# FFN up projections: 512-column matmuls over high and low activations, halves added on ACT and DVE

## The reference, cut to what matters

```
def swiglu(x, w_gu, w_down):
    g, u = jnp.split(x @ w_gu, 2, axis=-1)
    return (jax.nn.silu(g) * u) @ w_down
...
h = x + 0.5 * swiglu(rmsnorm(x, g[0]), w_ffn_gu[layer, 0], w_ffn_down[layer, 0])
```

## Time and profile before

| | |
|---|---|
| median of 3 runs | 2766.53 us (2764.23 to 2768.34) |
| span of the profiled execution | 2765.9 us |
| PE, PEld busy | 95%, 93% of the span |
| DVE, ACT busy | 66%, 45% |
| matmuls and weight loads | 21248 each |
| weight units | 407, 1 MB each |

### The profile page before, as it was taken

One profiled execution on the slowest core, in us unless ns is written; L12 is line 12 of the kernel. 1 busy time (PEld: TensorE's weight loads), 2 busy tenths in 40 slices (PEclk: granted clock), 3 DMA queues, 4 the chain that ended last, 5 costly groups with the idle time before them and its releaser, 6 DMA issues.

```text
span 2765.9 us, 49966 instructions
## 1 busy us (share of the span) xinstructions
PE 2638.7 (95%) x21248; PEld 2574.0 (93%) x21248; DVE 1820.8 (66%) x2256; ACT 1257.7 (45%) x1323; POOL 5.2 (0%) x13
## 2 busy tenths in 40 slices
PE   8999799999999999999969999999899999899998
PEld 8999799999999999999959999999899998778897
DVE  6567875576566755865676567557876586566565
ACT  4446554454444544544555445446454445333443
POOL 0000000000000000000000000000000000000000
PEclk9999999999999999999989999999999999999999
DMA  7554145545542555455415544554145544123251
GB/s 289 182 182 172 34 174 194 183 161 188 182 174 100 187 183 182 152 197 183 156 61 187 182 168 179 184 182 158 59 172 198 182 168 173 61 91 138 77 183 46
DMA packets 60204, 435.78 MB, mean 158 GB/s; under 512 B 6720, under 2 KB 6848, under 8 KB 7584
## 3 DMA queue, kind: packets, MB, share of 16 engines
q1 hardware_dynamic: 59184, 429.05, 43.3%
q0 software_dynamic: 880, 4.65, 0.5%
HBM read 432.63 MB, written 1.05 MB: 157 GB/s over the span
## 4 chain that ended last, share of the span: by engine, by line
PE 84%; DVE 12%; ACT 2%; issue 1%; DMA 0%; ACTq 0%; DVEq 0%
PE ps L596 56%; PE ps L623 18%; PE ps L609 4%; DVE w_lo L1349 2%; ACT w_hi L996 1%; PE ps L852 1%; DVE xg_lo L1392 1%; PE ps L832 1%; DVE xg_hi L1389 1%; PE ps L842 1%; DVE x L1453 1%; DVE scratch L1623 1%; DVE scratch L1779 1%; DVE scratch L1635 1%; DVE scratch L1613 0%
## 5 line engine op out<-in xcount | busy, mean ns | idle before, releaser
L1349 DVE TENSOR_TENSOR w_lo<-raw,w_hi 128x2048 fp32r<-128x2048 f32 x407 | 932.1, 2291 | 505.1 <-ACT w_hi L996 504.3
L596 PE MATMUL ps<-xg_hi,w_hi 128*128 128x256 f32 x4240 | 1212.5, 286 | 29.2 <-DVE xg_lo L1392 24.7
L596 PE MATMUL ps<-xg_hi,w_lo 128*128 128x256 f32 x4240 | 1201.1, 283 | 0.0
L596 PE MATMUL ps<-xg_lo,w_hi 128*128 128x256 f32 x4240 | 1201.0, 283 | 0.0
L996 ACT CAST w_hi<-raw 128x2048 fp32r<-128x2048 f32 x407 | 772.4, 1898 | 491.9 <-PE ps L623 248.0
L596 PEld LDWEIGHTS ps<-xg_hi,w_hi 128*128 128x128 f32 x4240 | 808.1, 191 | 38.5 <-issue 23.4
L596 PEld LDWEIGHTS ps<-xg_hi,w_lo 128*128 128x128 f32 x4240 | 808.4, 191 | 2.9 <-issue 2.4
L596 PEld LDWEIGHTS ps<-xg_lo,w_hi 128*128 128x128 f32 x4240 | 808.3, 191 | 0.0
L623 PE MATMUL ps<-mo_hi,w_hi 128*128 128x256 f32 x1568 | 445.1, 284 | 3.7 <-DVE xg_hi L1389 3.7
L623 PE MATMUL ps<-mo_hi,w_lo 128*128 128x256 f32 x1568 | 443.9, 283 | 0.0
L623 PE MATMUL ps<-mo_lo,w_hi 128*128 128x256 f32 x1568 | 443.8, 283 | 0.0
(11 more groups left out here) (260 smaller groups left out, 2339.4 us busy)
## 6 DMA issues: line engine op xcount, KB each, us to landing
raw<-weights_dram SPq DMA_DIRECT2D x407, 1024.0 KB, 4.8
scratch<-c_second_dram POOLq DMA_DIRECT2D x1, 1280.0 KB, 5.7
x<-x_t_dram SPq DMA_DIRECT2D x1, 1024.0 KB, 7.4
scratch<-p_t_dram POOLq DMA_DIRECT2D x4, 256.0 KB, 3.1
scratch<-mem_t_dram POOLq DMA_DIRECT2D x1, 1024.0 KB, 6.6
out_dram<-x SPq DMA_DIRECT2D x2, 512.0 KB, 2.6
common<-c_common_dram POOLq DMA_DIRECT2D x1, 640.0 KB, 8.5
scratch<-c_levels_dram POOLq DMA_DIRECT2D x1, 448.0 KB, 7.7
```

Source lines behind the costliest of these rows:

```text
L596: last = nc.tensor.matmul(bank(e)[:, half * T:(half + 1) * T], l, r, start=(k == 0 and j == 0 and half == 0), stop=(k == KC - 1 and j == 2 ...
L1349: V.tensor_tensor(w_lo[:, m % SPLIT, :], raw[:, m % RAW, :], w_hi[:, m % SPLIT, :].bitcast(F32), ALU.subtract).then_inc(weights_split, 1)
```

## The change

Before, each 128x128 piece of the weights takes three weight loads and three 256-column matmuls into one region of a bank. Now `xg_hi` and `xg_lo` are one tile `xg` with high and low side by side, and the high weights take one 512-column matmul over both; the low weights take a 256-column matmul over the high activations. The first half of the bank then holds high times high, the second half the two cross terms, so gate and up take a bank each. On the way out ACT copies the cross halves of both banks to SBUF, DVE adds the other halves (128x512), which frees the banks, and DVE multiplies by rstd (128x512). `sw` takes 12 banks in place of 11, so that pairs stay aligned; its token projection gives back two. Down units and all other phases keep their three passes.

```diff
-    "ffn": dict(units=HCH + STEPS, banks=HCH, norms=1, resid=KC, hidden=HCH, acc=3),
+    "ffn": dict(units=HCH + STEPS, banks=2 * HCH, norms=1, resid=KC, hidden=HCH, acc=3),
...
-        xg_hi = sb("xg_hi", [P, KC, T], F32R)
-        xg_lo = sb("xg_lo", [P, KC, T], F32R)
+        xg = sb("xg", [P, KC, 2, T], F32R)
+        xg_hi, xg_lo = xg[:, :, 0, :], xg[:, :, 1, :]
...
+            def project_up(n, e, operand_ready=None, dn=0, de=0):
+
+                pe.wait_ge(weights_split, n + 1 + dn)
+                pe.wait_ge(bank_read, e + 2 + de)
+                for k in range(KC):
+                    if operand_ready:
+                        pe.wait_ge(operand_ready[0], operand_ready[1] + k + 1)
+                    for half in range(2):
+                        o = bank(e + half)
+                        wc = slice(k * 256 + half * P, k * 256 + (half + 1) * P)
+                        nc.tensor.matmul(o, w_hi[:, n % SPLIT, wc], xg[:, k].rearrange("p a t -> p (a t)"),
+                                         start=(k == 0), stop=False, skip_group_check=True)
+                        last = nc.tensor.matmul(o[:, T:2 * T], w_lo[:, n % SPLIT, wc], xg[:, k, 0],
+                                                start=False, stop=(k == KC - 1), skip_group_check=True)
+                last.then_inc(weights_used, 1)
...
-                project(n0, e0, XG, (xg_ready, x0))
-                project(n0 + 1, e0 + 1, XG)
+                project_up(n0, e0, (xg_ready, x0))
+                project_up(n0 + 1, e0 + 2)
                 norm_sums(i)
-                project(n0 + 2, e0 + 2, XG)
-                project(n0 + 3, e0 + 3, XG)
+                project_up(n0 + 2, e0 + 4)
+                project_up(n0 + 3, e0 + 6)
...
                 def up(j, n, dn=0, dh=0, turn=0, early=False):
-                    act.wait_ge(up_scaled, h0 + j + 1 + dh)
-                    nc.scalar.activation(FFN_T[:, 2 + j % 2], FFN_T[:, j % 2], ACT.Silu).then_inc(silu_ready, 1)
+                    b = (e0 + 2 * j) % BANKS
+                    act.wait_ge(weights_used, n + 1 + dn)
+                    nc.scalar.copy(FFN_X[j % 2], ps[:, b:b + 2, T:2 * T]).then_inc(cross_ready, 1)
                     if not early:
                         high(n + SPLIT, dn, turn)
+                    act.wait_ge(up_scaled, h0 + j + 1 + dh)
+                    nc.scalar.activation(FFN_S[:, j % 2], FFN_Y[j % 2][:, 0], ACT.Silu).then_inc(silu_ready, 1)
...
                 def up(j, n, dn=0, dh=0, early=False):
-                    e = e0 + j
-                    dve.wait_ge(weights_used, n + 1 + dn)
-                    V.tensor_tensor(FFN_T[:, j % 2], pair(e)[:, 0], rstd[:], ALU.mult).then_inc(up_scaled, 1)
-                    V.tensor_tensor(FFN_T[:, 4 + j % 2], pair(e)[:, 1], rstd[:], ALU.mult).then_inc(bank_read, 1)
-                    dve.wait_ge(bank_read, e + 5 + dh)
-                    dve.wait_ge(silu_ready, h0 + j + 1 + dh)
-                    V.tensor_tensor(FFN_H[:, j % 2], FFN_T[:, 2 + j % 2], FFN_T[:, 4 + j % 2],
-                                    ALU.mult).then_inc(hidden_value, 1)
+                    b = (e0 + 2 * j) % BANKS
+                    cross, value = FFN_X[j % 2], FFN_Y[j % 2]
+                    dve.wait_ge(cross_ready, h0 + j + 1 + dh)
+                    V.tensor_tensor(cross, ps[:, b:b + 2, 0:T], cross, ALU.add).then_inc(bank_read, 2)
+                    dve.wait_ge(bank_read, e0 + 2 * j + 6 + 2 * dh)
+                    V.tensor_tensor(value, cross, row(rstd[:], 2), ALU.mult).then_inc(up_scaled, 1)
                     if not early:
                         low(n + SPLIT, dn)
+                    dve.wait_ge(up_scaled, h0 + j + 1 + dh)
+                    dve.wait_ge(silu_ready, h0 + j + 1 + dh)
+                    V.tensor_tensor(FFN_H[:, j % 2], FFN_S[:, j % 2], value[:, 1], ALU.mult).then_inc(hidden_value, 1)
                     dve.wait_ge(hidden_hi, h0 + j + 1 + dh)
```

More of the change, by code:

```diff
@@ L50 @@
     "ml": dict(units=16, banks=16, norms=1, resid=KC, ml=1),
-    "sw": dict(units=11, banks=11, norms=1, resid=KC, sw=1),
+    "sw": dict(units=11, banks=12, norms=1, resid=KC, sw=1),
     "second": dict(units=56, banks=50, norms=1, resid=KC, second=1),
@@ L338, in build @@
         rstd_ready = sem("rstd_ready")
+        cross_ready = sem("cross_ready")
         up_scaled = sem("up_scaled")
@@ L386, in build @@
         SQ_SUM = S[:, UNIT:UNIT + T]
-        FFN_T = chunks(UNIT + T, 6)
-        FFN_H = chunks(UNIT + 7 * T, 2)
+        FFN_X = [chunks(UNIT + T + 2 * i * T, 2) for i in range(2)]
+        FFN_Y = [chunks(UNIT + 5 * T + 2 * i * T, 2) for i in range(2)]
+        FFN_S = chunks(UNIT + 9 * T, 2)
+        FFN_H = chunks(UNIT + 11 * T, 2)
         PLE_P = chunks(6 * UNIT, 2)
@@ L663, in ffn @@
                     for s in (2, 3):
-                        project(n0 + 3 * s - 1, e0 + 2 * s, XG, dn=6 * it, de=4 * it)
-                        project(n0 + 3 * s, e0 + 2 * s + 1, XG, dn=6 * it, de=4 * it)
+                        project_up(n0 + 3 * s - 1, e0 + 4 * s, dn=6 * it, de=8 * it)
+                        project_up(n0 + 3 * s, e0 + 4 * s + 2, dn=6 * it, de=8 * it)
                         down(s - 1, n0 + 3 * s + 1, dn=6 * it, dh=4 * it)
                 s = STEPS - 1
-                project(n0 + 3 * s - 1, e0 + 2 * s, XG)
-                project(n0 + 3 * s, e0 + 2 * s + 1, XG)
+                project_up(n0 + 3 * s - 1, e0 + 4 * s)
+                project_up(n0 + 3 * s, e0 + 4 * s + 2)
                 down(s - 1, n0 + 3 * s + 1)
@@ L886, in sw @@
                 sums(5)
-                pe.wait_ge(bank_read, e0 + 7 + 4)
+                pe.wait_ge(bank_read, e0 + 8 + 4)
                 groups = quad_groups(SW_QK, SW_QK[:, 8:12], SW_V, SW_KV, True)
@@ L891, in sw @@
                 attention(att_before(i), groups, ATT_SW, read="bias")
-                w_out(i, n0 + 7, e0 + 7)
+                w_out(i, n0 + 7, e0 + 8)
             def banks_clear(g):
@@ L1019, in ffn @@
             def ffn(i):
-                n0, h0 = at(i, "units"), at(i, "hidden")
+                n0, e0, h0 = at(i, "units"), at(i, "banks"), at(i, "hidden")
                 norm(i, n0 + SPLIT)
                 def up(j, n, dn=0, dh=0, turn=0, early=False):
-                    act.wait_ge(up_scaled, h0 + j + 1 + dh)
-                    nc.scalar.activation(FFN_T[:, 2 + j % 2], FFN_T[:, j % 2], ACT.Silu).then_inc(silu_ready, 1)
+                    b = (e0 + 2 * j) % BANKS
+                    act.wait_ge(weights_used, n + 1 + dn)
+                    nc.scalar.copy(FFN_X[j % 2], ps[:, b:b + 2, T:2 * T]).then_inc(cross_ready, 1)
                     if not early:
                         high(n + SPLIT, dn, turn)
+                    act.wait_ge(up_scaled, h0 + j + 1 + dh)
+                    nc.scalar.activation(FFN_S[:, j % 2], FFN_Y[j % 2][:, 0], ACT.Silu).then_inc(silu_ready, 1)
                     act.wait_ge(hidden_value, h0 + j + 1 + dh)
@@ L1398, in scale, with scale_tokens @@
                 V.tensor_tensor(dst, pair(e), row(rstd[:], 2), ALU.mult).then_inc(bank_read, 1)
-            def scale_tokens(n, e, dst, col):
+            def scale_tokens(n, e, dst, col, banks=1):
                 dve.wait_ge(weights_used, n + 1)
@@ L1404, in scale_tokens @@
                     ins = V.tensor_scalar(dst[:, b], pair(e)[:, b], rcol[:, col + b:col + b + 1], None, ALU.mult)
-                ins.then_inc(bank_read, 1)
+                ins.then_inc(bank_read, banks)
             def columns(i):
@@ L1825, in sw @@
                     low(n0 + u + SPLIT)
-                scale_tokens(n0 + 6, e0 + 6, SW_V, 0)
+                scale_tokens(n0 + 6, e0 + 6, SW_V, 0, banks=2)
                 low(n0 + 6 + SPLIT)
```

2 lines of the change are left out of this document (1 added, 1 removed).

## The result

The changed kernel is slower: 2795.9 us (median of 4 runs, 2793.8 to 2801.8) against 2767.4 before on the same chip, ratio 1.0104 with a 95% interval of 1.0091 to 1.0116. The forecast was 2746, faster, with a range of 2725 to 2772.

A forecast was written before the change was run, and what follows sets the result against it. PE was taken as the bound, its up projections standing on a 120.4 ns weight-load floor. From 2765.9, minus 67.5 for merging, plus 32.0 waiting, 13 clock and 2.8 FFN ends, came 2746 us, range 2725 to 2772.

The forecast's parts named there:

- the first term of the sum: Up projections: a 512- plus a 256-column matmul takes 336.4 ns against 361.2 for three, gaining 67.5 us.
- a weight load without cover: Up projections: a weight load hides under 213 ns of streaming but not under 106.5, setting a 120.4 ns floor.
- the excess is a toll on every matmul: Rival, up projections: 13.9 ns paid per load and not hidden; pair 347.3 ns, 37.8 us gained, 2776; chance 0.12.
- neither rows 5 nor rows 6 show it: Argument against the toll: 256-column matmuls at the lower clock and f32 matmuls at 216 ns show no 13.9 ns.
- The wait at each FFN's start: Up 2, behind the norm's matmul, waits for up 0's banks: 4.0 us per FFN, 32 us in eight.
- The clock: Behind the gap at each FFN's start: two in three lose the full clock, 2.5 us each, 13 us.
- End of each FFN: ACT's chain for the last up unit, 5.75 us against 5.4, delays the next operand chain: 2.8 us in eight.
- What costs nothing: In the loop, added ACT and DVE work stays covered: PE's step 16.5 us against their 14.8.
- The two units behind ple: After the three ple phases, two up units gain nothing, since the norm's matmul waits for DVE's reduction.
- the 3 us that I named as a sign: PE's waits for `xg_lo`, 24.7 us in all before, would grow by 3 us if the forecast was right.

The follow-up runs named there:

- three_passes: Changed kernel with the 512-column matmul taken apart into two of 256, a weight load each; 2814.7 us, ratio 1.0169.
- the series of 96: Separate kernel running only series of 96 matmuls on PE, by type and width; 96 f32 matmuls left 192 records, 215.7 ns per record.
- grouped: Changed kernel, all sixteen 512-column matmuls of an up unit before its sixteen of 256, except unit 0 of an FFN; 2779.5 us, ratio 1.0046.
- half_grouped: Changed kernel with up matmuls ordered two of 512 columns, then two of 256, in all units; 2780.0 us, ratio 1.0045.
- ahead_late: Changed kernel, units 0 and 1 copied and summed before rstd and DVE's weight subtraction, unit 1's hidden chunk before its weight cast; 2769.3 us.
- best: Changed kernel with ahead_late and grouped together; 2755.4 us, ratio 0.9960 to the kernel before.

## Why the prediction was wrong

The step that failed is the first term of the sum, "A pair costs 336.4 ns where three cost 361.2". Measured: 353.4 (11.31 us / 32) where three cost 360. In place of 67.5 us the merging gave about 18 in my terms (6.6 ns x 16 x 170), and 19 by three_passes. With 18 in the sum, 2765.9 - 18 + 32.0 + 13 + 2.8 = 2796 against a span of 2792.4; with the other terms as they were measured, below, it is 2792.

It failed at one inference: that the extra 13.9 ns of the earlier trace rows were a weight load without cover. Both groups fit that, and they fit a toll of fp32r at the full clock as well. The earlier trace rows show that the extra is gone at the lower clock, and it is gone there for the change's pair too (640 ns), so they don't tell cover from toll. The earlier trace rows are f32 matmuls, which pay 2.4 ns per record, with a load as long as fp32r's. Their sixteen records are also eight instructions, as the series of 96 showed, and not the sixteen matmuls that I called them. I took the price of an fp32r instruction from another type because it had "the same columns, the same load and the same clock". The rival "the excess is a toll on every matmul" was right in mechanism; I gave it 0.12 and wrote that "neither rows 5 nor rows 6 show it", where rows 6 could not have shown it. Its own size was still 6.6 ns a pair short, since no row of before had two widths in turns, and so was its time: 2776. A small part of the 361.2 was reading: 17.34 us per step came from two casts of ACT, while PE's own steps are 17.28 us apart, 120.0 ns per matmul.

The other terms, by the same steps:

- **The wait at each FFN's start**, 4.0 us: up 2 starts 4.28 us after the norm's matmul (4.38 behind ple), 4.04 later than before, 32.3 in eight. The profile's gap is 3.68, forecast 3.7.
- **The clock**, 13 us: up 2 and up 3 take 12.7 to 12.9 us behind the gap where two warm units take 11.31, summed over eight 12 us. The sum was right by luck, through two errors: all eight gaps lost the clock, not two in three, and each cost 1.4 to 1.6 us and not 2.5, as the clock was back 3.2 to 4.1 us after up 2 began, not after 5.3 us of work. The 2.5 is a real price, but of a longer loss that the change happened not to meet: among the 24 such gaps of three_passes, grouped and half_grouped seven cost 2.3 to 2.7 us each.
- **End of each FFN**, 2.8 us: nothing. From the last two down units to the next norm's matmul PE takes the same time as before to 0.02 us. I had the chain at 5.75 us against a unit of 5.4; it takes 5.49 (copy at 105.03, the cast to `mo_hi` ends at 110.52), the unit 5.65, and ACT stands idle for 0.17 before the next copy. The last down unit does start later, by 0.45 us and not 0.9, and costs nothing, as forecast.
- **What costs nothing**: right. PE waits for no weights and for no bank inside the loop; in the steady loop it waits for neither ACT nor DVE.
- **The two units behind ple**: right, nothing is gained in them. From up 0 to the norm's matmul PE takes 14.44 us, before 14.45. Its waits for the low half of `xg` did not grow by the 3 us that I named as a sign: 19.7 and 4.0 us (two lines) against the 24.7 of the earlier trace rows.

## What to carry to other kernels

Price an instruction that the trace doesn't have from the same type, not from the same number of columns: fp32r, f32 and bf16 differ here in what they pay per matmul. When two readings of a cost give different prices for the edit, give them chances by what the rows can tell apart, and ask whether the row would have looked different under the rival.

Before a ring of buffers is halved, look for the place where the readers wait for something behind the writers: here eight waits of 4 us stood at the one point where ACT's order put the copy behind rstd, and they and the clock that they cost ate more than twice the gain. Moving work ahead of a wait can push out what was hidden in that wait, such as a table load.

## What I had not expected of the hardware

- At the full clock an fp32r matmul with its load costs columns at 2.4 GHz plus 13.3 ns: 120.0, 146.7, 173.3, 226.7 ns for 256, 320, 384, 512 columns. At the lower clock it pays none of it: 213 ns for 256 columns, 640 for a pair. bf16 pays 2.5 and f32 2.4 per record, at two records per f32 instruction.
- Two widths in single turns cost 6.6 ns more per pair in fp32r; in twos 1.7; in bf16 nothing.
- Gaps of 3.68 us between dense stretches lost the clock 32 times in 32, gaps of 2.19 three times in six, gaps of 2.04 to 2.08 (ahead_late, best) six times in ten, and the six of 1.34 to 1.45 never. In the change a loss cost 1.4 to 1.6 us, in other runs up to 2.7.
